# A two-block transformer kernel: memory tokens loaded in five parts between weights, zeros through TensorE first, modulation pieces moved between engines, constants in two loads

## The chip, the cores and the metric

The kernel runs on one core of a Trainium2 chip. The metric is the device time of one execution in microseconds. Three runs of the kernel before took 1735.03, 1736.86 and 1738.09 us; the median is 1736.86 us.

## What is computed

The reference is two transformer blocks over a sequence of 256 positions and 2048 features, in float32. The first block has adaptive modulation, then a wide projection, stick-breaking attention, retention, and an output projection. The second block has two layers that both attend to 256 memory tokens. What the change touches is this:

```
mod = silu(c) @ w_ada + b_ada              # c: (1, 2048), w_ada: (2048, 6144)
shift, scale, gate = split(mod, 3)
h = rms_norm(x, norm_gain) * (1 + scale) + shift
proj = h @ w_in
...
mem_n = rms_norm(mem, mem_norm_w)          # mem: (256, 2048)
k, v = mem_n @ w_mk, mem_n @ w_mv          # for both layers, width 512 each
```

The key and value products of the memory tokens depend on nothing else, so the kernel computes them first, while the modulation of the first block is being formed.

## The kernel before

Activations lie transposed: 16 tiles of 128 features by 256 positions. Every product is done in two parts of reduced float32: a matrix w is split into w_hi (ScalarE's copy, L429) and w_lo = w - w_hi (VectorE's subtraction, L433), and the activations likewise. Weights arrive in chunks of 512 KB, loaded by SyncE's queue (`load_weights`, L417) into a ring of 7 slots; a slot is loaded again when the chunk seven before it has been used. ScalarE and VectorE split a chunk three chunks ahead of TensorE (AHEAD = 3), and w_hi has 5 slots. `run_split` is the loop of ScalarE and VectorE over the chunks of a product, with a hook per chunk in which other work stands; `run_products` is TensorE's. When a block of a product ends, ScalarE copies its first half out of PSUM and VectorE adds the second (`take_product`, `add_product`); both wait there until TensorE has done the block's last chunk. Nothing is reordered: each engine executes its list as written, and semaphores tie the lists.

The first stage is G_MEM, four products of the memory tokens with 8 chunks each, so 32 chunks. The first and third have chunks of 2 tiles by 512 columns, and the weights are the moving side (L497 to L499, 12 matmuls of 512 columns a chunk); the second and fourth have chunks of 4 tiles by 256 columns, and the tokens are the moving side (L503 and L505). A unit u is the hook behind chunk u. On ScalarE and VectorE unit u comes after the split of chunk u + 3, on TensorE after the matmuls of chunk u.

Beside it run these:

- Memory tokens. SyncE loads them in four parts of four feature tiles (512 KB each), the first before weight 0, the others behind weights 0, 1 and 3; the constants (512.5 KB) come behind weight 4. ScalarE scales them by the gain (`mem_hi`, L808), VectorE makes the low parts (`mem_lo`, L1342). The first four tiles are made ahead of the first three splits, the others in units 0, 2 and 4. The root of the mean square is applied at the end, from sums: ScalarE squares four tiles at a time (`norm_square`, L712; units 0, 1, 3, 5), POOL sums three of the four groups (`add_squares`, L618 to L622), and TensorE sums over the partitions in unit 6 (`sum_squares`, L1998, L2002). The third and fourth squares wait for the POOL group two before them to be free.
- Modulation. For half 0, 32 pieces of w_ada (128 by 1024, 512 KB) are loaded by POOL's queue (L640) into a ring of 6 slots. A slot is loaded again once its piece has been used. VectorE multiplies a piece by its element of silu(c) and adds it to a sum (`ada_add`, L1332 for the first of each sum, L1335). Pieces 22, 23, 30 and 31 (DIRECT) go another way: TensorE multiplies them by a one-column operand in units 21, 22, 26 and 27 (`direct_columns`, L2022). VectorE adds one piece per unit from unit 3 to 27, and a second one in units 8, 13 and 18. In unit 28 TensorE turns the two sums into columns (`modulation_columns`, L2009).
- x. POOL loads x in four parts before pieces 10, 12, 14 and 16. ScalarE squares it in units 17, 19, 21 and 23; POOL sums before it issues pieces 22, 25 and 28; TensorE sums in unit 25; the inverse root is made in unit 26. In units 29, 30 and 31 ScalarE and VectorE make the first eight tiles of h (`half_norm`; on VectorE L1377 and L1378 for the modulation, L1226 for a tile's product, L1235 for its low part, on ScalarE L738 for the high part).

The next stage, 40 chunks, multiplies those eight tiles with w_in while the other half's 32 pieces come in. Its first two chunks need tiles 0 to 3.

## Time and profile before

| | |
|---|---|
| Median of three runs | 1736.86 us |
| The profiled execution | 1735.74 us |
| Its span | 1733.7 us |
| TensorE busy | 1694.3 us, 98% |
| VectorE busy | 1309.0 us, 76% |
| ScalarE busy | 905.9 us, 52% |
| GpSimd busy | 179.5 us, 10% |
| DMA | 357.00 MB, mean 206 GB/s |

Matmuls are pipelined, so a busy TensorE is not one at its peak: at half clock it is as busy as at full clock. The time of a matmul is the distance between the starts of two of them, not the duration in the row. In the timeline a row gives start, duration, engine, line, operation, output and inputs, shapes and count; the square brackets hold how long the engine was idle before it and which instruction or transfer ended that. Line numbers are those of the kernel before.

### The profile page before, as it was taken

Reading aid. Unit: us, or ns where it says so; the run is one execution under the profiler, and the core shown is the slowest. Engines: PE = TensorE matmul, PEld = TensorE weight load, DVE = VectorE, ACT = ScalarE, POOL = GpSimd, SP = SyncE. Lnnn points to the kernel's source line nnn. Section 1 sums busy time; section 2 is a strip of 40 time slices with the busy share of each in tenths; the row PEclk is TensorE's granted clock in tenths of the full one; section 3 lists DMA queues with packets and bytes.
Section 4 is the critical chain, followed back from the end, with each engine's and each line's share of the span. In section 5 each row is a group of like instructions: output and inputs, shape, how many; then the busy total and the mean of one; then the engine's idle time right before and its main releaser. Section 6 shows DMA issues by size and latency. Waiting matters only on the chain.

```text
span 1733.7 us, 24087 instructions
## 1 busy us (share of the span) xinstructions
PE 1694.3 (98%) x9511; PEld 1460.7 (84%) x9511; DVE 1309.0 (76%) x1633; ACT 905.9 (52%) x1178; POOL 179.5 (10%) x198
## 2 busy tenths in 40 slices
PE   7899999999999999999999999999999999999997
PEld 5788878888888888888888888888888888888886
DVE  6879999897798757887677779965566667778654
ACT  6344453445565446665445666744454455565543
POOL 4321101000110200111010010001111000000001
PEclk9999999999999999999999999999999999999999
DMA  9989979775555566667676556565666565444563
GB/s 354 384 301 342 349 239 325 257 259 152 159 166 182 185 192 185 192 183 220 175 226 195 160 168 172 185 192 186 190 190 183 170 197 144 135 140 127 171 193 110
DMA packets 312287, 357.00 MB, mean 206 GB/s; under 512 B 11632, under 2 KB 285168, under 8 KB 312176
## 3 DMA queue, kind: packets, MB, share of 16 engines
q1 hardware_dynamic: 295792, 296.24, 56.3%
q0 software_dynamic: 16384, 59.22, 9.9%
q8 instruction: 76, 1.25, 0.3%
q14 instruction: 35, 0.29, 0.1%
HBM read 353.29 MB, written 2.13 MB: 205 GB/s over the span
## 4 chain that ended last, share of the span: by engine, by line
PE 72%; DVE 15%; ACT 6%; issue 3%; DMA 2%; POOL 1%; SPq 0%; DVEq 0%; ACTq 0%
PE psG L503 40%; PE psG L505 20%; DVE w_lo L433 6%; ACT w_hi L429 3%; PE psG L497 2%; PE psG L499 2%; PE psG L498 2%; DMA raw<-in_mem_w 2%; DVE P L1282 1%; DVE P L1287 1%; PE psH L1992 1%; DVE W L1896 0%; PE psH L2022 0%; PE psH L2227 0%; DMA ada_ring<-in_w_ada 0%
## 5 line engine op out<-in xcount | busy, mean ns | idle before, releaser
L433 DVE TENSOR_TENSOR w_lo<-raw,w_hi 128x1024 fp32r<-128x1024 f32 (+1 forms) x560 | 691.5, 1247 | 203.9 <-ACT w_hi L429 202.2
L503 PE MATMUL psG<-xA,w_hi 128*128 128x512 f32 x2624 | 839.7, 401 | 3.2 <-ACT P L470 1.1
L429 ACT ACTIVATE w_hi<-raw 128x1024 fp32r<-128x1024 f32 (+1 forms) x560 | 569.1, 1041 | 215.4 <-PE psG L505 152.4
L505 PEld LDWEIGHTS psG<-xA,w_lo 128*128 128x128 f32 x2624 | 493.0, 188 | 114.8
L505 PE MATMUL psG<-xA,w_lo 128*128 128x256 f32 x2624 | 519.3, 278 | 0.0
L503 PEld LDWEIGHTS psG<-xA,w_hi 128*128 128x128 f32 x2624 | 404.0, 189 | 12.0 <-issue 6.5
L503 PE MATMUL psG<-yP,w_hi 128*128 128x512 f32 x960 | 302.2, 396 | 3.0 <-DVE P L1287 1.6
L505 PEld LDWEIGHTS psG<-yP,w_lo 128*128 128x128 f32 x960 | 180.4, 188 | 42.6
L505 PE MATMUL psG<-yP,w_lo 128*128 128x256 f32 x960 | 188.7, 278 | 0.0
L472 ACT ACTIVATE P<-psG 128x512 f32<-128x512 f32 (+2 forms) x103 | 60.8, 590 | 228.1 <-PE psG L505 228.1
L503 PEld LDWEIGHTS psG<-yP,w_hi 128*128 128x128 f32 x960 | 146.2, 189 | 3.7 <-DVE P L1287 1.8
L1282 DVE TENSOR_TENSOR P<-psG,P 128x512 f32<-128x512 f32 (+2 forms) x103 | 70.2, 682 | 101.9 <-ACT P L472 101.8
L618 POOL TENSOR_TENSOR W<-W 128x512 f32<-128x512 f32 x17 | 28.1, 1653 | 582.4 <-ACT W L712 582.3
L640 POOL DMA_DIRECT2D ada_ring<-in_w_ada x96 | 51.1, 533 | 295.2 <-DVE gate_sum L1335 115.6
L1335 DVE SCALAR_TENSOR_TENSOR ada_sum<-ada_ring,silc,ada_sum 128x1024 f32<-128x1024 f32 x56 | 75.3, 1348 | 0.0
L1307 DVE TENSOR_TENSOR xT<-psG,xT 128x512 f32<-128x512 f32 x30 | 20.7, 691 | 42.5 <-PE psG L505 42.0
L497 PE MATMUL psG<-w_hi,xA 128*128 128x512 f32 x128 | 51.4, 401 | 0.0
L499 PE MATMUL psG<-w_hi,xA 128*128 128x512 f32 x128 | 50.0, 390 | 0.0
L498 PE MATMUL psG<-w_lo,xA 128*128 128x512 f32 x128 | 49.9, 390 | 0.0
L503 PE MATMUL psG<-xQ,w_hi 128*128 128x512 f32 x144 | 45.3, 396 | 0.0
L497 PE MATMUL psG<-w_hi,xM 128*128 128x512 f32 x64 | 28.5, 445 | 14.2 <-DVE w_lo L433 11.7
L742 ACT ACTIVATE xA<-xT,vec 128x256 fp32r<-128x256 f32 x32 | 14.3, 501 | 51.6 <-DVE xT L1310 27.2
(352 smaller groups left out, 1752.2 us busy)
## 6 DMA issues: line engine op xcount, KB each, us to landing
raw<-in_w_in SPq DMA_DIRECT2D x360, 512.0 KB, 3.8
raw<-in_w_out SPq DMA_DIRECT2D x128, 512.0 KB, 3.5
ada_ring<-in_w_ada POOLq DMA_DIRECT2D x96, 512.0 KB, 6.4
raw<-in_mem_w SPq DMA_DIRECT2D x32, 512.0 KB, 10.6
raw<-in_w_uq SPq DMA_DIRECT2D x24, 384.0 KB, 3.4
raw<-in_w_ukv SPq DMA_DIRECT2D x32, 128.0 KB, 2.4
raw<-in_w_ukv SPq DMA_DIRECT2D x16, 256.0 KB, 3.3
P<-in_memT SPq DMA_DIRECT2D x4, 512.0 KB, 7.1
```

The costliest lines, as they stand in the source:

```text
L429: nc.scalar.activation(high(n), low(n, raw), ACT.Copy).then_inc(hi_ready, 1)
L433: nc.vector.tensor_tensor(low(n), low(n, raw), high(n), ALU.subtract).then_inc(lo_ready, 1)
L472: nc.scalar.activation(g.dst(b), product(g, b, 0), ACT.Copy).then_inc(copied, 1)
L497: nc.tensor.matmul(out, x_hi, hi[:, w], start=first, stop=False)
L498: nc.tensor.matmul(out, x_hi, lo[:, w], start=False, stop=False)
L499: last = nc.tensor.matmul(out, x_lo, hi[:, w], start=False, stop=end)
L503: nc.tensor.matmul(psG[:, bank + f, :], hi[:, w], x, start=first, stop=False)
L505: last = nc.tensor.matmul(psG[:, bank + f, S:2 * S], lo[:, w], x[:, 0:S], start=False, stop=end)
L618: pair(nc.gpsimd.tensor_tensor(a[:, 0:512], a[:, 0:512], a[:, 512:1024], ALU.add))
L640: pool.dma_start(ada_ring[slot][:, :], ada_rows(k, part, half)).then_inc(ada_loaded[slot], 16)
L1282: ins = v.tensor_tensor(out, product(g, b, 1), out, ALU.add)
L1335: v.scalar_tensor_tensor(out=out, in0=src, scalar=silc[:, k:k + 1], in1=out, op0=ALU.mult, op1=ALU.add).then_inc(ada_used, 1)
```

## The change

The memory tokens are loaded in five parts, of 2, 2, 4, 4 and 4 tiles; the first stands before weight 0 and one behind each of weights 0 to 3. ScalarE and VectorE make part 0, split chunk 0, make part 1, split chunk 1, make part 2, split chunk 2, make part 3; part 4 is made in unit 0. Only the first 256 of 1025 columns of the constants (ones and identity) are loaded behind weight 4; the others come behind con1, after the weights of G_SBQK. TensorE first runs 16 matmuls over a tile of zeros that VectorE sets. No piece goes directly through TensorE. ScalarE scales pieces 0 and 1 (the first of each sum) in unit 4; VectorE adds one piece per unit from unit 5 on and the last three behind the stage. ScalarE's squares of x stand in units 21, 23, 25 and 27, TensorE's sum in unit 30, the inverse root in unit 31. `modulation_columns` and the three steps of `half_norm` stand behind the stage. POOL's first issue waits for the load of tiles 8 to 11, as before, which is now the fourth part.

The diff, with a declaration of semaphore names left out:

```diff
@@ -72,6 +72,9 @@
...
 MEM_UNITS, EARLY_UNITS = 32, 40
+MEM_PIECES = (range(0, 2), range(2, 4), range(4, 8), range(8, 12), range(12, 16))
+SCALED_BY_ACT = 2
+WARM_UP = 16
 MEM_ROOT = 80
@@ -229,7 +232,7 @@
...
         loaded = {n: sem("loaded_" + n) for n in ("x", "vec", "con", "con1", "pos", "late")}
-        mem_loaded = [sem(f"mem_loaded{i}") for i in range(4)]
+        mem_loaded = [sem(f"mem_loaded{i}") for i in range(len(MEM_PIECES))]
         ada_loaded = [sem(f"ada_loaded{i}") for i in range(len(ADA_RING))]
@@ -237,7 +240,7 @@
...
             "rt_t0 rt_s rt_qk rt_D rt_z rt_at rt_o rt_os rt_vc rt_sq rt_var rt_ln rt_rs rt_y "
-            "f1_yz f1_y f1_hi f1_lo dt_step ada_direct ada_folded mem_col mem_k "
+            "f1_yz f1_y f1_hi f1_lo dt_step ada_folded mem_col mem_k "
             "cv_acc cv_tap cv_a cv_e cv_l cv_b cv_s cv_done xt xd_done "
@@ -368,16 +371,6 @@
...
         ADA_BEFORE = [max([i for i in range(m) if ADA_SLOT[i] == ADA_SLOT[m]], default=None) for m in range(3 * ADA_HALF)]
-        DIRECT = (22, 23, 30, 31)
-        ADA_ADDED = [m - sum(d < m for d in DIRECT) for m in range(3 * ADA_HALF + 1)]
-
-        def modulation_used(eng, m):
-
-            if m in DIRECT:
-                eng.wait_ge(q["ada_direct"], DIRECT.index(m) + 1)
-            else:
-                eng.wait_ge(ada_used, ADA_ADDED[m] + 1)
-
         ADA_COUNT = [ADA_SLOT[:m + 1].count(ADA_SLOT[m]) for m in range(3 * ADA_HALF)]
@@ -580,16 +573,20 @@
...
-            def load_memory(g):
-                sp.dma_start(mem_raw[:, 4 * g:4 * g + 4, :], io["memT"].rearrange("(t p) s -> p t s", p=NP)[:, 4 * g:4 * g + 4, :])\
-                  .then_inc(mem_loaded[g], 16)
+            early_con = slice(0, CON["rot64"])
+            late_con = slice(CON["rot64"], NCON)
+
+            def load_memory(i):
+                part = slice(MEM_PIECES[i][0], MEM_PIECES[i][-1] + 1)
+                sp.dma_start(mem_raw[:, part, :], io["memT"].rearrange("(t p) s -> p t s", p=NP)[:, part, :])\
+                  .then_inc(mem_loaded[i], 16)
...
-                if c in (0, 1, 3):
-                    load_memory((0, 1, 3).index(c) + 1)
+                if c < 4:
+                    load_memory(c + 1)
                 if c == 4:
-                    sp.dma_start(con[:, :], io["con"]).then_inc(loaded["con"], 16)
+                    sp.dma_start(con[:, early_con], io["con"][:, early_con]).then_inc(loaded["con"], 16)
@@ -597,6 +594,8 @@
...
                     sp.dma_start(con1[:, :], io["con1"]).then_inc(loaded["con1"], 16)
+                    sp.wait_ge(loaded["con"], 16)
+                    sp.dma_start(con[:, late_con], io["con"][:, late_con]).then_inc(loaded["con"], 16)
             out = io["out"].rearrange("(t p) s -> p t s", p=NP)
@@ -623,7 +622,7 @@
...
             X_QUARTERS = (10, 12, 14, 16)
-            pool.wait_ge(mem_loaded[2], 16)
+            pool.wait_ge(mem_loaded[3], 16)
             for m, (half, k, part) in enumerate(ADA_ORDER):
@@ -633,7 +632,7 @@
...
                 if ADA_BEFORE[m] is not None:
-                    modulation_used(pool, ADA_BEFORE[m])
+                    pool.wait_ge(ada_used, ADA_BEFORE[m] + 1)
                 if m in X_QUARTERS:
@@ -670,6 +669,7 @@
...
             landed(pool, G_CB)
+            pool.wait_ge(loaded["con"], 32)
             pool.dma_start(C("dup", S), io["con"][:, CON["dup"]:CON["dup"] + S]).then_inc(loaded["late"], 16)
@@ -784,10 +784,6 @@
...
-            def first():
-                for n in range(AHEAD):
-                    split_hi(act, n)
-
             def run(g, hook=no_hook, hook_first=True, before_taken=lambda: None):
@@ -801,10 +797,10 @@
...
-            def mem_hi(g):
-
-                act.wait_ge(mem_loaded[g], 16)
-                for t in range(4 * g, 4 * g + 4):
+            def mem_hi(i):
+
+                act.wait_ge(mem_loaded[i], 16)
+                for t in MEM_PIECES[i]:
                     f(xM[:, t, 0:S], mem_raw[:, t, :], ACT.Copy, scale=V("mem_norm", t)).then_inc(q["nm_hi"], 1)
@@ -814,23 +810,32 @@
...
-            mem_hi(0)
-            first()
+            for i in range(AHEAD):
+                mem_hi(i)
+                split_hi(act, i)
+            mem_hi(AHEAD)
+
+            def first_scaled(m):
+
+                act.wait_ge(ada_loaded[ADA_SLOT[m]], 16 * ADA_COUNT[m])
+                act.wait_ge(q["silc_step"], 2)
+                f(ada_sum[:, m, :], ada_ring[ADA_SLOT[m]][:, :], ACT.Copy, scale=silc[:, 0:1]).then_inc(ada_used, 1)
             def mem_hook_1(unit):
-                if unit in (0, 2, 4):
-                    mem_hi(unit // 2 + 1)
+                if unit == 0:
+                    mem_hi(AHEAD + 1)
                 if unit in (0, 1, 3, 5):
                     norm_square(0, (0, 1, 3, 5).index(unit), mem_raw)
+                if unit == 4:
+                    for m in range(SCALED_BY_ACT):
+                        first_scaled(m)
                 if unit == 7:
                     mem_root()
-                if unit in (17, 19, 21, 23):
+                if unit in (21, 23, 25, 27):
                     act.wait_ge(loaded["x"], 64)
-                    norm_square(1, (17, 19, 21, 23).index(unit), xT)
-                if unit == 26:
+                    norm_square(1, (21, 23, 25, 27).index(unit), xT)
+                if unit == 31:
                     norm_inverse_root(1)
-                if unit >= MEM_UNITS - 3:
-                    half_norm(0, unit - (MEM_UNITS - 3))
@@ -848,6 +853,8 @@
...
                 run(g, at_units(8 * i, mem_hook_1), hook_first=False)
+            for step in range(3):
+                half_norm(0, step)
             for i, g in enumerate((G_SBQK0, G_RTQK0, G_SBV0)):
@@ -877,7 +884,7 @@
...
             act.wait_ge(loaded["con1"], 16)
-            run(G_RTV, lambda b, p: sb_hook(2 + b, p), before_taken=lambda: act.wait_ge(ada_used, ADA_ADDED[3 * ADA_HALF]))
+            run(G_RTV, lambda b, p: sb_hook(2 + b, p), before_taken=lambda: act.wait_ge(ada_used, 3 * ADA_HALF))
@@ -1259,10 +1266,6 @@
...
                 return hook
-
-            def first():
-                for n in range(AHEAD):
-                    split_lo(dve, n)
@@ -1314,6 +1317,7 @@
...
+            link(v.memset(fold_to[:, :], 0.0))
             dve.wait_ge(q["silc_step"], 1)
@@ -1331,19 +1335,21 @@
...
                 else:
-                    dve.wait_ge(ada_used, ADA_ADDED[m] - (m < 2 * ADA_HALF))
+                    dve.wait_ge(ada_used, max(SCALED_BY_ACT, m - (m < 2 * ADA_HALF)))
                     v.scalar_tensor_tensor(out=out, in0=src, scalar=silc[:, k:k + 1], in1=out, op0=ALU.mult,
...
-            def mem_lo(g):
-
-                for t in range(4 * g, 4 * g + 4):
+            def mem_lo(i):
+
+                for t in MEM_PIECES[i]:
                     dve.wait_ge(q["nm_hi"], t + 1)
...
-            mem_lo(0)
-            first()
+            for i in range(AHEAD):
+                mem_lo(i)
+                split_lo(dve, i)
+            mem_lo(AHEAD)
@@ -1390,34 +1396,36 @@
...
                     if units == MEM_UNITS:
-                        done.append(done[-1] + (3 <= u < units - 4) + (u in (8, 13, 18)))
+                        done.append(done[-1] + (u >= 5))
                     else:
...
-            ADDED_0 = [m for m in range(ADA_HALF) if m not in DIRECT]
-
             def ada_hook(u0, units, half):
...
                         u = u0 + 8 * b + p // 2
-                        if units == MEM_UNITS and u in (0, 2, 4):
-                            mem_lo(u // 2 + 1)
+                        if units == MEM_UNITS and u == 0:
+                            mem_lo(AHEAD + 1)
                         for m in range(done[u], done[u + 1]):
-                            ada_add(ADA_HALF * half + m if half else ADDED_0[m])
+                            ada_add(ADA_HALF + m if half else SCALED_BY_ACT + m)
                         if half and u == 1:
...
                         if half and u == units - 5:
-                            dve.wait_ge(ada_used, ADA_ADDED[2 * ADA_HALF])
+                            dve.wait_ge(ada_used, 2 * ADA_HALF)
                             fold(ada_sum.rearrange("p c n -> p (c n)"), 2)
-                        if u >= units - 3:
+                        if half and u >= units - 3:
                             half_norm(half, u - (units - 3))
...
                 run(g, ada_hook(8 * i, MEM_UNITS, 0), hook_first=False)
+            for m in range(SCALED_BY_ACT + ada_units(MEM_UNITS)[-1], ADA_HALF):
+                ada_add(m)
+            for step in range(3):
+                half_norm(0, step)
             for i, g in enumerate((G_SBQK0, G_RTQK0, G_SBV0)):
@@ -1430,7 +1438,7 @@
...
             def gate_fold(half):
-                dve.wait_ge(ada_used, ADA_ADDED[2 * ADA_HALF + KT * (half + 1)])
+                dve.wait_ge(ada_used, 2 * ADA_HALF + KT * (half + 1))
                 fold(gate_sum[:, :], 1)
@@ -1669,6 +1677,7 @@
...
             run(G_SZ1, xdt_hook)
+            dve.wait_ge(loaded["con"], 32)
@@ -2011,29 +2020,21 @@
...
-            def direct_columns(i):
-
-                m = DIRECT[i]
-                half, k, part = ADA_ORDER[m]
-                pe.wait_ge(ada_loaded[ADA_SLOT[m]], 16 * ADA_COUNT[m])
-                pe.wait_ge(q["silc_step"], 2)
-                for t in range(8):
-                    c = KT * part + t
-                    ins = mm(psH[:, BD, c:c + 1], ada_ring[ADA_SLOT[m]][:, t * NP:t * NP + NP], silc[:, k:k + 1],
-                             start=i == 0 and t == 0, stop=False)
-                ins.then_inc(q["ada_direct"], 1)
+            def warm_up():
+
+                pe.wait_ge(dve_step, 1)
+                for _ in range(WARM_UP):
+                    mm(psH[:, BD, 0:NP], fold_to[:, :], fold_to[:, :], start=True, stop=True)
             def modulation_columns():
-                pe.wait_ge(ada_used, ADA_ADDED[ADA_HALF])
-                ada_columns(ada_sum[:, 0, :], 0, None, first=False)
+                pe.wait_ge(ada_used, ADA_HALF)
+                ada_columns(ada_sum[:, 0, :], 0, None)
                 ada_columns(ada_sum[:, 1, :], KT, "ada_cols", first=False)
...
                 mm(psH[:, BD, 0:32 * parts], fold_to[:, :], folded[:, 0:32 * parts], start=True, stop=True).then_inc(q[name], 1)
-
-            DIRECT_AT = (21, 22, 26, 27)
@@ -2048,15 +2049,13 @@
...
                     ins.then_inc(q["mem_col"], 1)
-                if u == 25:
+                if u == 30:
                     sum_squares(1)
-                if u in DIRECT_AT:
-                    direct_columns(DIRECT_AT.index(u))
-                if u == MEM_UNITS - 4:
-                    modulation_columns()
-
+
+            warm_up()
             for i, g in enumerate(G_MEM):
                 run_products(pe, g, lambda b, p: mem_tail_hook(i, p))
+            modulation_columns()
```

## Rows read from the trace of the kernel before

**Rows 1.** Busy time by stretch: stretch, length, engines with counts, PEclk, DMA share, GB/s.

```profile
9.43:25.81 16.38, 13.91 (x49) 10.89 (x49) 9.31 (x12) 11.48 (x17) 9.06 (x10) 0.99 1.06 385
...
40.93:127.72 86.79, 81.95 (x458) 70.47 (x459) 68.28 (x64) 36.37 (x45) 29.93 (x40) 0.98 0.97 350
127.72:239.35 111.63, 110.82 (x610) 95.46 (x609) 104.63 (x113) 51.34 (x63) 15.33 (x29) 1.00 0.95 323
```

**Rows 2.** Timeline of TensorE, first matmuls of chunks 8, 16, 24 and 32.

```profile
40.79 0.72 PE L503 MATMUL psG<-xM,w_hi 128*128 128x512 f32 x2
...
63.18 0.40 PE L497 MATMUL psG<-w_hi,xM 128*128 128x512 f32 x1
...
96.13 0.61 PE L503 MATMUL psG<-xM,w_hi 128*128 128x512 f32 x2
...
127.72 0.63 PE L503 MATMUL psG<-xA,w_hi 128*128 128x512 f32 x2
```

**Rows 3.** Timeline of TensorE, sums, waits and one-column passes.

```profile
35.54 0.59 PE L1998 MATMUL psH<-W,con 128*128 128x256 f32 x2
...
37.51 0.58 PE L497 MATMUL psG<-w_hi,xM 128*128 128x512 f32 x1
...
79.77 0.47 PE L497 MATMUL psG<-w_hi,xM 128*128 128x512 f32 x1 [0.90 <-DVE w_lo L433]
...
85.34 2.13 PE L2022 MATMUL psH<-silc,ada_ring 128*128 128x1 f32 x16 [2.58 <-DMA ada_ring<-in_w_ada]
...
91.56 1.84 PE L2022 MATMUL psH<-silc,ada_ring 128*128 128x1 f32 x16
...
115.79 3.63 PE L2009 MATMUL psH<-con,ada_sum 128*128 128x1 f32 x32
```

**Rows 4.** Timeline of TensorE, the first start and one restart.

```profile
9.43 0.76 PE L497 MATMUL psG<-w_hi,xM 128*128 128x512 f32 x1 [9.43 <-DVE w_lo L433]
...
15.42 0.40 PE L499 MATMUL psG<-w_hi,xM 128*128 128x512 f32 x1
...
25.81 0.80 PE L497 MATMUL psG<-w_hi,xM 128*128 128x512 f32 x1 [2.47 <-DVE xM L1342]
...
28.95 0.40 PE L498 MATMUL psG<-w_lo,xM 128*128 128x512 f32 x1
```

**Rows 5.** Timeline of ScalarE, splits of chunks 0, 5 and 19.

```profile
6.97 1.06 ACT L429 ACTIVATE w_hi<-raw 128x1024 fp32r<-128x1024 f32 x1 [0.17 <-DMA raw<-in_mem_w]
...
22.06 1.06 ACT L429 ACTIVATE w_hi<-raw 128x1024 fp32r<-128x1024 f32 x1 [2.38 <-DMA raw<-in_mem_w]
...
69.65 1.06 ACT L429 ACTIVATE w_hi<-raw 128x1024 fp32r<-128x1024 f32 x1 [2.24 <-DMA raw<-in_mem_w]
```

**Rows 6.** Timeline of all engines, squares of the memory tokens and their sums.

```profile
16.58 1.04 ACT L712 ACTIVATE W<-P 128x1024 f32<-128x1024 f32 x1
...
26.69 2.13 POOL L618 TENSOR_TENSOR W<-W 128x512 f32<-128x512 f32 x1 [0.58 <-ACT W L712]
...
30.05 1.61 POOL L622 TENSOR_TENSOR W<-W 128x256 f32<-128x256 f32 x1
...
31.69 1.06 ACT L712 ACTIVATE W<-P 128x1024 f32<-128x1024 f32 x1 [1.59 <-POOL W L622]
```

**Rows 7.** Timeline of VectorE and ScalarE, what the end is made of.

```profile
60.39 2.48 DVE L1335 SCALAR_TENSOR_TENSOR ada_sum<-ada_ring,silc,ada_sum 128x1024 f32<-128x1024 f32 x2
...
111.41 0.60 ACT L472 ACTIVATE memkv<-psG 128x512 f32<-128x512 f32 x1 [5.57 <-PE psG L505]
...
119.86 1.28 DVE L1226 SCALAR_TENSOR_TENSOR W<-xT,gs,W 128x256 f32<-128x256 f32 x3
```

**Rows 8.** Timeline of POOL and VectorE, one group of sums beside an add.

```profile
75.49 1.38 POOL L618 TENSOR_TENSOR W<-W 128x512 f32<-128x512 f32 x1 [1.51 <-ACT W L712]
75.64 2.31 DVE L1335 SCALAR_TENSOR_TENSOR ada_sum<-ada_ring,silc,ada_sum 128x1024 f32<-128x1024 f32 x1
...
78.49 0.57 POOL L640 DMA_DIRECT2D ada_ring<-in_w_ada x1
```

## The prediction

> **What bounds the kernel now.** I read the table of stretches first. From 127.72 us on TensorE is busy for 110.82 of 111.63 us, and the change hardly reaches that part: it moves later or earlier as a whole. Between 9.43 and 127.72 us, the memory products, TensorE has gaps while the 16 DMA engines are at a share of about 1.0 and move 385 GB/s in the first stretch [rows 1]. Then TensorE's timeline, to see where its time goes. The stage is 32 chunks of weights. I number them 0 to 31; chunk 8 starts at 40.79, chunk 16 at 63.18, chunk 24 at 96.13, and the stage ends at 127.72 us [rows 2]. A chunk without disturbance takes 22.39 / 8 = 2.80 us (chunks 8 to 15); a token-major one takes 12 matmuls of 0.228 us = 2.73 us.
>
> From 40.79 to 127.72 are 86.9 us for 24 chunks that need 8 x 2.80 + 8 x 2.73 + 8 x 2.80 = 66.6 us. The other 20.3 us are seen in the rows: four groups of one-column matmuls on modulation pieces (2.0 us, then 1.7 us each: 7.1), the 32 one-column passes that finish the sums (from 115.79, 3.63 in the row, 3.5 up to the next start), the sum of squares of x (2.0, as the one at 35.54 to 37.51), a wait of 2.7 us for a modulation piece before 85.34 with a slow restart behind it (1.6), and three short waits for weights, 0.6 to 0.9 us each (the last is shown), a little more in start-to-start time [rows 3]. Before 40.79: the first 13 matmuls run at 0.43 us against 0.23 us (512 columns at 1.2 and at 2.4 GHz, though the granted clock of the stretch reads 0.99; 2.7 us lost), a gap 22.95 to 25.81 (2.6 us), and 7 slow matmuls behind it (1.4 us) [rows 4].
>
> **The change part by part.**
>
> *Start.* The first load is 256 KB less, 0.7 us at 385 GB/s (512 KB: 1.36 us). Weight 0 was waited for until 6.97 us [rows 5], now about 6.3, and chunk 0 starts at 8.7 instead of 9.43. The sum of squares at 35.54, ten passes of 256 columns, takes 0.20 us a pass; so the 16 matmuls on zeros, two passes of 128 columns each, take 0.4 us apiece at the low clock and last some 6 us from about 1 us on. The low clock lasted 6.0 us after the first start (9.43 to 15.42, rows 4). I let the clock be high at 8.7, worth 2.7 us; at worst nothing is won. Chunks 1 to 6 then follow the landings: by pieces in SP's order, weight 5 is behind 10.25 pieces and 2 of POOL's instead of 11 and 2, so 21 instead of 22.06 us [rows 5]. With split (1.06) and subtraction (1.23) chunk 5 starts at 23.4, chunk 6 ends at 29.2 instead of 35.5 us.
>
> There TensorE must sum the squares of the memory tokens, and this is late next. The chain is ScalarE square, POOL sums, square, sums. POOL's third group began at 26.69, its last sum ended at 31.66, and the last square ran 31.69 to 32.75 [rows 6]. The first square waits in the new kernel for the load of tiles 12 to 15 and falls at 17.1 against 16.58 us; POOL's groups and the issues between them keep their order, so the third group again starts near 26.7. ScalarE's two scalings (2 x 1.04) stand between the third square and the fourth and fit into that POOL group. So the end of chunk 6 is followed by 2.5 us of idle to 31.7, then sums at the low clock (3.4 + 1.0 in place of 2.0 us), done 36.1; chunk 7 with a slow head: 3.1; the columns of the root 0.35: chunk 8 at 39.6, a gain of 1.2 us. The warm start's 2.7 us is spent in this wait. Bounds for the part: chain 1 us later and longer low clock, -0.5; chain done when TensorE arrives, +6.5 (chunk 8 at 34.3).
>
> *Middle.* The four pieces leave TensorE: 7.1 us, and the 2.7 + 1.6 us at 85 go with the wait for a piece. VectorE gets them less the two that ScalarE scales: 2 x 1.24 us, and adds one piece per chunk; split and add are 1.2 + 1.24 against 2.80 us. Are weights in time? By pieces: weight 19 was waited for until 69.65 [rows 5]. SP had queued 25 pieces to it, and POOL 4 of x and, by the code's slot rule (a slot is free when the piece six before it has been added; VectorE had added 15), some 19.7; 48.7 x 1.36 + 3.9 = 70.1. New: 24.25 + 4 + 17.7 = 45.95, so 66.4 + 2.3 for splitting = 68.7. TensorE gets to chunk 19 at 39.6 + 8 x 2.80 + 3 x 2.73 = 70.2. So the weights no longer hold it, with 1.5 us to spare, and the short waits go (2.6). From there a chunk asks for two pieces, 2.72 us. Chunk 31 ends at 39.6 + 66.6 + 2.0 (squares of x) = 108.2 us. Bound above: weights late by 2 us.
>
> *End.* Before, the final columns and the first part of x's normalization stood between chunks 28 and 31, and TensorE had three chunks to do. Now all of it stands behind chunk 31, bare. With T its end: ScalarE copies the last block (0.2 + 0.6), VectorE adds it (T + 1.5), then three pieces left over at 1.24 (60.39, two in 2.48) [rows 7]: T + 5.2. The columns at the low clock, 2.0/1.7 of 3.5 = 4.0: T + 9.2. VectorE's 0.4 for modulation, then three scalings in 1.28 and five more steps of 0.40 up to the low part of tile 3 [rows 7]: 4.5, T + 13.7. TensorE starts the next stage there, slow for half of its first 3 to 6 us, 1.4 to 2.8 lost (rows 4); I take 2.2. VectorE will be somewhat behind at T, since the pieces 22, 25 and 28 wait in POOL's queue behind x's squares, whose ScalarE units are 4 later: +0.7. Together 16.6 us against nothing.
>
> 108.2 + 16.6 = 124.8 against 127.72: 2.9 us gained.
>
> *Nothing for the rest.* The memset of zeros (under 0.3 us) is ahead of VectorE's wait for ScalarE. The constants in two loads take 0.75 of a piece from the beginning and put it, with SP's wait for the first load (long landed), behind con1's load, where 1.0 us of transfer meets weights that are up to seven chunks ahead: 0, at worst 1.0. POOL and VectorE wait for the second load several stages later; nothing stands behind those waits by then. POOL's first issue waits for the third long load, one piece later, 1.4 us; the squares come after it anyhow.
>
> *Clock.* The rows show full speed regained after 3.1 us in one place and 6.0 in another [rows 4]. The Trainium skill ("TensorE: Matmul & The Clock Gate", "What's actually happening") says that the point varies from run to run, one kernel having had 6, 11 or 14 slow matmuls. By its 6 to 14 a restart costs, as an estimate, 1.2 to 2.8 us at this kernel's 0.2 us each; with two new restarts the sum would be between 1 us better and 1 us worse. The two restarts in the rows have 7 and 13, and agree.
>
> **The rivals.** (a) *The squares are not late*, or the low clock is not entered in so short a wait. For: POOL's sums are shorter when VectorE is idle. Then weights bind: chunk 19 at 68.7, T = 106.7; 106.7 + 13.7 + 2.2 = 122.6, 5.1 us gained: 1731.8 for the measured median. (b) *VectorE is behind at the end: slower.* An add beside POOL's sums took 2.31 us for 1.24 (75.49 and 75.64) [rows 8]. POOL's second and third group for x, up to 5.0 us each (26.69 to 31.66, rows 6), come while VectorE has chunks 25 to 31 to do, after piece 22, which took from 78.49 to 85.3 to be there [rows 3, 8]. If each of six units costs 1.2 + 2.31 = 3.5 for 2.44, VectorE loses 6.4 us against a slack of about 1: 5.4 us later at T, and TensorE's start with it: 108.2 + 13.7 + 5.4 + 2.2 = 129.5, 1.8 us slower, 1738.7. It decides once the last of the three adds ends over 8.8 us after T (5.2 + 3.6). Against: POOL sums only half of that time. The Trainium skill ("GPSIMD Engine Reference", "Specifications") has VectorE instructions with two SBUF inputs contend with GpSimd, as these adds have; by it the case is real for all adds beside sums, and the trace agrees with 2.31 us. (c) *The change does not free TensorE*, since transfers hold it throughout: every piece still has to come, only 3 pieces fewer by chunk 19 (4 us). For: share 1.0 for 90 us. With weights 2 us late from there and the same end: 110.2 + 16.6 = 126.8, 0.9 us gained, 1736.0.
>
> **How the numbers follow.** The profiled execution took 1735.74 us, 2.0 around the span of 1733.7; the sum makes it 1732.8. The median of the three runs is 1.12 above it, 1736.86, so the forecast is 1734.0. Forecast 0.50, (a) 0.20, (b) 0.15, (c) 0.15. What can be told from no change is 0.2%, 3.5 us: faster needs 1733.4 or less. The forecast lies near that edge, and 0.4 of it falls beyond (0.20); (a) is beyond for nearly all of it (0.18), (c) hardly (0.02): faster 0.40. Slower than 1740.4 is (b) for half of it (0.08) and 0.02 of what I have not seen: 0.10. Same: 0.50. Own range of the forecast 1731.5 to 1737; with (a) and most of (b) 1728.5 to 1739.
>
> **What would show it.** Chunk 0 near 8.7 us at 0.23 us a matmul; a gap of TensorE after 29 us until POOL's and ScalarE's squares at 31.7, with slow matmuls behind; chunk 8 near 39.6; no wait for a weight over 0.5 us from there to chunk 31, end near 108; then about 14 us with nothing but 4 us of one-column passes, and the next stage at 122.6 with slow first matmuls; from there all rows as before, 3 us earlier. Wrong would be: chunk 8 before 36 (a), VectorE's last add later than 116 (b), waits for weights in chunks 16 to 25 (c), or a changed length from the next stage to the end.

## The result, and the profile after

The changed kernel takes 1741.01 us (median of 14 runs) against 1736.94 us for the kernel before (14 runs on the same chip): a ratio of 1.0022, interval 1.0014 to 1.0029. It is 4.1 us, 0.2%, slower; the forecast was 1734.0 us, 2.9 us faster. In a second set of runs, of the unchanged files, it was 1741.83 against 1737.38 us, 1.0027 (1.0017 to 1.0036). One execution of the changed kernel had a granted clock of 0.65 from end to end and took 2398.96 us; it is left out, and the profile shown here is of an execution in the second set.

Its page, the span and the busy times:

```profile
span 1738.9 us, 24035 instructions
...
PE 1697.5 (98%) x9479; PEld 1463.2 (84%) x9479; DVE 1311.2 (75%) x1636; ACT 908.2 (52%) x1180; POOL 179.8 (10%) x198
```

The span is 5.2 us longer than the 1733.7 us of before. The table of stretches of the changed kernel, columns as in [rows 1]: the first loads, the last eight chunks of the memory products, the end of that stage, and the stage behind it.

```profile
9.43:30.00 20.57, 20.43 (x84) 16.75 (x84) 14.82 (x21) 15.88 (x24) 11.66 (x12) 0.92 1.07 378
84.00:108.00 24.00, 22.88 (x126) 19.56 (x125) 24.00 (x18) 13.41 (x16) 16.52 (x17) 1.00 1.07 375
108.00:130.00 22.00, 10.16 (x49) 9.58 (x48) 14.85 (x23) 4.33 (x10) 3.17 (x6) 0.66 0.65 238
130.00:240.00 110.00, 109.18 (x590) 94.02 (x589) 100.53 (x105) 48.28 (x58) 15.33 (x29) 0.97 0.92 316
```

The reader sees three things. From 84 to 108 us VectorE has no idle time at all (24.00 of 24). From 108 to 130 us TensorE is busy for 10.16 of 22 us, at a granted clock of 0.66; before, it was busy from 108 us to the end of the stage, 127.72, at full clock. From 136 us on hardly anything differs: span less start of the next stage is 1733.7 - 127.72 = 1606.0 us before and 1738.9 - 129.52 = 1609.4 us after, and 2.8 of the 3.4 us more lie in the first 6 us of it: the matmuls that take from 129.52 to 135.60 in the rows below took 3.3 us before. So nearly the whole question lies ahead of 136 us. TensorE's timeline of the changed kernel, the rows that answer to [rows 2 to 4]:

```profile
1.05 6.11 PE L2027 MATMUL psH<-fold_to 128*128 128x128 f32 x32 [1.05 <-DVE fold_to L1320]
9.57 0.76 PE L490 MATMUL psG<-w_hi,xM 128*128 128x512 f32 x1 [2.41 <-DVE w_lo L426]
...
12.69 0.40 PE L491 MATMUL psG<-w_lo,xM 128*128 128x512 f32 x1
...
31.90 0.67 PE L2007 MATMUL psH<-W,con 128*128 128x256 f32 x2 [1.54 <-POOL W L621]
32.90 3.56 PE L2011 MATMUL psH<-W,con 128*128 128x256 f32 x8 [0.33 <-ACT W L712]
...
39.51 0.72 PE L496 MATMUL psG<-xM,w_hi 128*128 128x512 f32 x2
...
61.90 0.40 PE L490 MATMUL psG<-w_hi,xM 128*128 128x512 f32 x1
...
84.22 0.62 PE L496 MATMUL psG<-xM,w_hi 128*128 128x512 f32 x2
...
90.33 0.70 PE L496 MATMUL psG<-xM,w_hi 128*128 128x512 f32 x2 [0.38 <-DVE w_lo L426]
...
110.30 0.40 PE L498 MATMUL psG<-xM,w_lo 128*128 128x256 f32 x2
117.94 6.99 PE L2018 MATMUL psH<-con,ada_sum 128*128 128x1 f32 x32 [7.24 <-DVE ada_sum L1339]
129.52 1.19 PE L496 MATMUL psG<-xA,w_hi 128*128 128x512 f32 x2 [4.60 <-issue]
...
134.77 0.99 PE L496 MATMUL psG<-xA,w_hi 128*128 128x512 f32 x2
135.60 0.40 PE L498 MATMUL psG<-xA,w_lo 128*128 128x256 f32 x2
```

Chunk 8 starts at 39.51, chunk 16 at 61.90, chunk 24 at 84.22 us: TensorE is then 11.9 us ahead of before (96.13, [rows 2]). Chunk 31 ends at 110.70 us (110.30 + 0.40), 17.0 us ahead of the 127.72 of before, since the columns and two of the one-column pieces no longer stand in front of its end. From there TensorE does nothing but 32 one-column passes until 129.52 us, and the first matmuls of the next stage, up to 135.60, run at half speed. The 17.0 us and 4.6 more are given back behind chunk 31: 18.8 us up to the next stage and 2.8 us at its slow head.

VectorE's timeline of the changed kernel behind chunk 31, and one pair of rows from the stretch ahead of it:

```profile
87.23 1.87 POOL L617 TENSOR_TENSOR W<-W 128x512 f32<-128x512 f32 x1
87.87 2.32 DVE L426 TENSOR_TENSOR w_lo<-raw,w_hi 128x1024 fp32r<-128x1024 f32 x1
...
112.42 1.27 DVE L1339 SCALAR_TENSOR_TENSOR ada_sum<-ada_ring,silc,ada_sum 128x1024 f32<-128x1024 f32 x1
113.62 0.68 DVE L1285 TENSOR_TENSOR memkv<-psG,memkv 128x512 f32<-128x512 f32 x1
114.22 3.66 DVE L1339 SCALAR_TENSOR_TENSOR ada_sum<-ada_ring,silc,ada_sum 128x1024 f32<-128x1024 f32 x3
124.96 0.17 DVE L1383 TENSOR_TENSOR mod<-psH,vec 128x16 f32<-128x16 f32 x1 [7.08 <-PE psH L2018]
...
125.37 1.28 DVE L1233 SCALAR_TENSOR_TENSOR W<-xT,gs,W 128x256 f32<-128x256 f32 x3
```

VectorE has three instructions to finish when TensorE ends (the add that began at 110.09, the subtraction behind it and the add at 112.42), so the block's add, which waits for TensorE alone, starts only at 113.62. Then the three pieces left over, then it waits 7.08 us for the columns.

### The profile page after: what moved, and what is told of

It reads as the page before. It is cut to its first block, busy times and chain, and to the rows that moved or that the text cites. A ratio compares the mean times of both kernels' runs of the same rounds, so it can differ in the third digit from the quotient of the medians.

```text
span 2397.0 us, 24035 instructions
## 1 busy us (share of the span) xinstructions
PE 2373.3 (99%) x9479; PEld 1801.4 (75%) x9479; DVE 1314.5 (55%) x1636; ACT 911.9 (38%) x1180; POOL 165.8 (7%) x198
## 4 chain that ended last, share of the span: by engine, by line
PE 99%; DVE 0%; issue 0%; DMA 0%; ACT 0%; SPq 0%; DVEq 0%
PE psG L496 54%; PE psG L498 27%; PE psG L491 3%; PE psG L490 3%; PE psG L492 3%; PE psH L2001 1%; PE psH L2192 0%; PE psH L2213 0%; PE psH L2294 0%; PE psH L2226 0%; PE psH L2293 0%; PE psH L2305 0%; PE psH L2095 0%; PE psH L2018 0%; PE psH L2194 0%
## 5 line engine op out<-in xcount | busy, mean ns | idle before, releaser
L496 PE MATMUL psG<-xA,w_hi 128*128 128x512 f32 x2624 | 1114.1, 514 | 5.4 <-issue 4.6
L498 PEld LDWEIGHTS psG<-xA,w_lo 128*128 128x128 f32 x2624 | 543.6, 207 | 282.6 <-issue 54.2
L498 PE MATMUL psG<-xA,w_lo 128*128 128x256 f32 x2624 | 670.5, 344 | 0.0
L496 PEld LDWEIGHTS psG<-xA,w_hi 128*128 128x128 f32 x2624 | 513.6, 221 | 24.7 <-issue 14.9
L496 PE MATMUL psG<-yP,w_hi 128*128 128x512 f32 x960 | 399.8, 507 | 0.0
L498 PEld LDWEIGHTS psG<-yP,w_lo 128*128 128x128 f32 x960 | 198.9, 207 | 104.1 <-issue 19.2
L498 PE MATMUL psG<-yP,w_lo 128*128 128x256 f32 x960 | 244.1, 344 | 0.0
L496 PEld LDWEIGHTS psG<-yP,w_hi 128*128 128x128 f32 x960 | 187.2, 221 | 0.2
L490 PE MATMUL psG<-w_hi,xA 128*128 128x512 f32 x128 | 66.4, 518 | 0.0
L492 PE MATMUL psG<-w_hi,xA 128*128 128x512 f32 x128 | 65.0, 508 | 0.0
L496 PE MATMUL psG<-xM,w_hi 128*128 128x512 f32 x128 | 53.6, 509 | 0.0
```

The costliest lines, as they stand in the source:

```text
L490: nc.tensor.matmul(out, x_hi, hi[:, w], start=first, stop=False)
L492: last = nc.tensor.matmul(out, x_lo, hi[:, w], start=False, stop=end)
L496: nc.tensor.matmul(psG[:, bank + f, :], hi[:, w], x, start=first, stop=False)
L498: last = nc.tensor.matmul(psG[:, bank + f, S:2 * S], lo[:, w], x[:, 0:S], start=False, stop=end)
```

## The experiments

All runs are of one core and in rounds against the kernel before, whose median was 1736.9 to 1737.4 us in each set. In short, with the start of the next stage (the first matmul on xA) and whether that is at full speed. The last two columns are of one profiled execution each, which was up to 2.8 us faster (e6) and up to 1.5 us slower (e10) than the median, so differences of 1 to 2 us between two rows of them show little by themselves:

| kernel | median us | ratio to before (interval) | next stage at | its speed |
|---|---|---|---|---|
| before | 1736.94 | 1 | 127.72 | full |
| e1: the changed kernel | 1741.83 | 1.0027 (1.0017 to 1.0036) | 129.52 | half |
| e2: before, bare end | 1742.67 | 1.0031 (1.0020 to 1.0042) | 130.79 | half |
| e3: changed, no zeros | 1740.83 | 1.0019 (1.0009 to 1.0028) | 130.83 | half |
| e4: before, new loads | 1737.63 | 1.0002 (0.9992 to 1.0011) | 127.92 | full |
| e5: changed, zeros at the end | 1737.85 | 1.0005 (0.9997 to 1.0014) | 126.56 | full |
| e6: changed, end inside | 1733.43 | 0.9979 (0.9970 to 0.9989) | 121.93 | full |
| e7: changed, no pieces left over | 1738.84 | 1.0008 (0.9999 to 1.0017) | 126.35 | half |
| e8: changed, squares of x early | 1741.81 | 1.0029 (1.0017 to 1.0040) | 131.13 | half |
| e9: e7 with zeros | 1735.72 | 0.9991 (0.9983 to 1.0000) | 127.29 | full |
| e10: e6, second adds later | 1735.22 | 0.9989 (0.9980 to 0.9998) | 128.03 | full |
| e11: before, no one-column pieces | 1732.60 | 0.9973 (0.9962 to 0.9984) | 123.15 | full |
| e12: e11, ScalarE scales two | 1735.08 | 0.9989 (0.9978 to 1.0001) | 125.15 | full |

Span less start of the next stage is 1606.0 to 1607.7 us for all that start it at full speed, and up to 3.7 us more for the others.

**e1: the changed kernel again.**

> The changed kernel as it is, for its profile. Theory A (the bare end is dearer than predicted): chunk 31 of the memory products ends near 108 us, but the next stage starts at 126 to 130 us, behind a gap of 18 us or more; everything before is as forecast. Theory B (the gain before the end is missing): chunk 31 ends at 112 us or later, the gap is 14 to 16 us. Theory C (a later stage pays): the next stage starts at 122 to 124 us as forecast, and the loss of 4 us stands behind it, in the 40 chunks with the other half's pieces or where the rest of the constants is loaded.

Measured: 1741.83 us; its rows are those above. The loss is repeated. It is theory A, with some of B: the gap behind chunk 31 is 18.8 us and the next stage starts at 129.52 us, and chunk 31 is 2.5 us late. Theory C fell.

**e2: the kernel before with the bare end alone.**

```diff
-                if unit >= MEM_UNITS - 3:
-                    half_norm(0, unit - (MEM_UNITS - 3))
...
                 run(g, at_units(8 * i, mem_hook_1), hook_first=False)
+            for step in range(3):
+                half_norm(0, step)
...
-                if u == MEM_UNITS - 4:
-                    modulation_columns()
...
                 run_products(pe, g, lambda b, p: mem_tail_hook(i, p))
+            modulation_columns()
```

> The kernel before, with only the columns of the modulation and the first eight tiles of h moved behind the memory products. Theory A: slower by 10 us or more (nothing earlier is gained, the end is bare: columns 0.5 us dearer, 4.5 us of VectorE's first tiles, 2 to 3 us of low clock, wait for the last block's copy and add 1.5 us), some 9 to 12 us. Theory C: the same 9 to 12 us. If the end is cheaper than I think, under 6 us.

Measured: 5.3 us more than before, 1.0031 (1.0020 to 1.0042) of it. That is not the 9 to 12 us expected, but its last case, an end cheaper than thought, under 6 us. It has TensorE's timeline

```profile
122.56 3.63 PE L2011 MATMUL psH<-con,ada_sum 128*128 128x1 f32 x32
130.79 1.19 PE L503 MATMUL psG<-xA,w_hi 128*128 128x512 f32 x2 [4.60 <-issue]
```

Here the pieces are all added when TensorE arrives, so the columns follow at once and at full speed (3.63 us). Still 4.60 us of idle follow, VectorE's and ScalarE's first tiles, and then a start at half speed. So a bare end without late adds and without slow columns costs 5.3 us here: more than the whole forecast gain.

**e3: the changed kernel without the 16 matmuls on zeros.**

```diff
-            warm_up()
             for i, g in enumerate(G_MEM):
```

> The changed kernel without the 16 matmuls on zeros. By the prediction the warm start is spent in the wait for the squares of the memory tokens, so nothing changes: within 1 us of the changed kernel. The rival, that the start is worth its 2.7 us, has it 2.5 to 3 us slower than the changed kernel.

Measured: 1740.83 us, 1.0 us less than with the zeros, and the intervals overlap: the zeros bring nothing. TensorE's timeline:

```profile
8.56 0.77 PE L490 MATMUL psG<-w_hi,xM 128*128 128x512 f32 x1 [8.56 <-DVE w_lo L426]
...
31.63 0.67 PE L2007 MATMUL psH<-W,con 128*128 128x256 f32 x2 [0.96 <-POOL W L621]
32.63 1.99 PE L2011 MATMUL psH<-W,con 128*128 128x256 f32 x8 [0.33 <-ACT W L712]
...
37.55 0.72 PE L496 MATMUL psG<-xM,w_hi 128*128 128x512 f32 x2
```

The sum waits for POOL at 31.63 us as it did at 31.90 with the zeros. The next eight passes took 1.99 us, not 3.56, and chunk 8 starts 2.0 us earlier than in e1. That can't be put down to the missing zeros. The kernels e5 to e10 below have the zeros and the same code as e1 up to chunk 8. In e7, e9 and e10 the eight passes took 1.99 us as well, behind 1.84, 1.53 and 1.48 us of idle, and chunk 8 started at 37.62, 38.05 and 38.52 us. In e5, e6 and e8 they took 3.12, 3.68 and 3.65 us, behind 1.49, 1.88 and 1.51 us, and chunk 8 started at 39.10, 39.81 and 40.32 us. Which clock follows a wait of this length changes from one execution to the next. In e3 the 2.0 us are gone again by the end of the stage (next stage at 130.83 us): TensorE waits 3.9 us for VectorE's low parts between 40 us and the end, against 1.1 in e1. What the runs show is that the sum waits for POOL with the zeros and without them, so a warm start has nothing to gain up to there.

**e4: the kernel before with the new loads alone** (five parts between the weights, constants in two loads; the fifth part shares the semaphore of con1).

```diff
+MEM_PIECES = (range(0, 2), range(2, 4), range(4, 8), range(8, 12), range(12, 16))
...
-                if c in (0, 1, 3):
-                    load_memory((0, 1, 3).index(c) + 1)
+                if c < 4:
+                    load_memory(c + 1)
...
-            mem_hi(0)
-            first()
+            for i in range(AHEAD):
+                mem_hi(i)
+                split_hi(act, i)
+            mem_hi(AHEAD)
```

> The kernel before, with only the five loads of memory tokens, their order on ScalarE and VectorE, and the constants in two loads; one load's semaphore is shared with a later one. By the prediction the squares come at the same time and the sum waits for them, so the gain is 0 to 1.5 us. Rival: the transfers saved (0.75 of a piece, 1 us) and the earlier start carry through to 4 us, since weights bind in chunks 16 to 22. Rival on the other side: the late constants cost 1 us where con1 is loaded.

Measured: 1.0002 (0.9992 to 1.0011). The new order of loads is worth nothing by itself, and costs nothing.

**e5: the changed kernel with zeros around the columns.** 30 zero matmuls ahead of the columns and 18 behind them; nothing is on TensorE's list there but the wait. VectorE overwrites the tile of zeros one unit later than in e1, since it is needed longer.

```diff
+            zeros(30, BD)
             modulation_columns()
+            zeros(18, BA)
```

> The changed kernel with 30 more matmuls on zeros between chunk 31 and the modulation columns and 18 between the columns and the next stage (and the tile of zeros overwritten one unit later). Theory A, the low clock at the bare end costs some 6.5 us (columns 7.0 instead of 3.5 us, first chunks of the next stage 3.1 us lost): columns in 3.5 us, next stage at full speed, 5 to 6.5 us faster than the changed kernel, about 1735.5. Rival, the waits themselves are the loss and the clock only a symptom of the trace: within 1 us of the changed kernel. Second rival, zeros do not raise the clock or are dropped in the wait of 4.6 us: 3.5 us at most.

Measured: 1737.85 us, 4.0 us less than e1, with the same work late on the same engines. TensorE's timeline:

```profile
109.93 6.86 PE L2031 MATMUL psH<-fold_to 128*128 128x128 f32 x60
117.32 3.73 PE L2018 MATMUL psH<-con,ada_sum 128*128 128x1 f32 x32 [0.53 <-DVE ada_sum L1339]
120.91 5.89 PE L2031 MATMUL psH<-fold_to 128*128 128x128 f32 x36
126.56 0.70 PE L496 MATMUL psG<-xA,w_hi 128*128 128x512 f32 x2
```

The columns take 3.73 us instead of 6.99, and the first matmuls of the next stage run at full speed. So 3.3 us in the columns and about 3 us at the head of the stage were the low clock alone; against that sum of 6.3 us the medians show 4.0. About 1.0 of the difference is that the last zeros are still running when the first tile is ready (120.91 + 4.60 = 125.5 us), for these 36 passes took 0.16 us each, partly at the low clock; the rest is not accounted for. The expectation, 5 to 6.5 us, was missed by 1 us.

**e6: the changed kernel with its end inside the stage again**: squares, root, columns and first tiles in the units of before, and seven second adds so that no piece is left over.

```diff
-                        done.append(done[-1] + (u >= 5))
+                        done.append(done[-1] + (5 <= u < 28) + (u in (8, 11, 14, 17, 20, 23, 26)))
...
-                        if half and u >= units - 3:
+                        if u >= units - 3:
                             half_norm(half, u - (units - 3))
...
+                if u == MEM_UNITS - 4:
+                    modulation_columns()
```

> The changed kernel with its end put back as it was before: squares of x in units 17 to 23, sum in 25, root in 26, columns in 28, the eight tiles in units 29 to 31; VectorE adds two pieces in seven units so that all are added by unit 27. Theory A, the move of the end behind the stage is the loss: the next stage starts at 116 to 120 us, 8 to 11 us faster than the kernel before, about 1727. Rival, VectorE (pieces it did not have before, beside POOL's sums) or the transfers can't deliver 32 pieces by then: the stage ends at 124 us or later, 1733 or more.

Measured: 1733.43 us, 8.4 us less than e1 and 0.9979 (0.9970 to 0.9989) of before: the loss becomes a gain. TensorE's timeline:

```profile
108.31 3.90 PE L2016 MATMUL psH<-con,ada_sum 128*128 128x1 f32 x32 [0.61 <-DVE ada_sum L1339]
...
121.93 0.63 PE L496 MATMUL psG<-xA,w_hi 128*128 128x512 f32 x2
```

All that the changed kernel lost was in where its end stands and in the pace of adds that goes with it; this run does not tell these two apart. The expectation, next stage at 116 to 120 us and 1727 us, was too good: in this trace TensorE waits 4.8 us for low parts on the way, and runs at the low clock for 3.4 us twice, once of it right behind the columns (from 112.08 us).

**e7: the changed kernel with no pieces left over**, the end still bare.

```diff
-                        done.append(done[-1] + (u >= 5))
+                        done.append(done[-1] + (5 <= u < 32) + (u in (13, 17, 21)))
```

> The changed kernel with the three leftover pieces added as second ones in units 13, 17 and 21, so that none stands behind the stage. If the leftover adds are on the path, 3.7 us less between chunk 31 and the columns, and 3 to 4 us faster than the changed kernel, about 1737.5. Rival, VectorE is behind anyhow from chunk 24 on and what it does not do at the end it does before: under 1 us.

Measured: 1738.84 us, 3.0 us less than e1, as expected if the adds were on the path; but the rows show another cause. TensorE's and VectorE's timelines:

```profile
114.89 0.40 PE L498 MATMUL psG<-xM,w_lo 128*128 128x256 f32 x2
117.43 4.32 PE L2018 MATMUL psH<-con,ada_sum 128*128 128x1 f32 x32 [2.15 <-DVE ada_sum L1339]
126.35 1.19 PE L496 MATMUL psG<-xA,w_hi 128*128 128x512 f32 x2 [4.60 <-issue]
```

```profile
116.10 1.27 DVE L1339 SCALAR_TENSOR_TENSOR ada_sum<-ada_ring,silc,ada_sum 128x1024 f32<-128x1024 f32 x1
117.30 0.68 DVE L1285 TENSOR_TENSOR memkv<-psG,memkv 128x512 f32<-128x512 f32 x1
```

The columns start at 117.43 us, hardly earlier than in e1 (117.94): chunk 31 now ends at 115.29 instead of 110.70, with 6.8 us of waits for VectorE's low parts against 1.1, since VectorE has three adds more to do before it. The adds are only moved; VectorE ends them at the same time. What is gained is the clock: TensorE idles 2.15 us ahead of the columns, not 7.24, and they take 4.32 us, not 6.99.

The same trace has the warm start that e1 lacked, and a sum of squares at full speed behind a longer wait than e1's 1.54 us:

```profile
8.58 0.47 PE L490 MATMUL psG<-w_hi,xM 128*128 128x512 f32 x1 [2.13 <-DVE w_lo L426]
8.88 0.40 PE L491 MATMUL psG<-w_lo,xM 128*128 128x512 f32 x1
...
31.69 0.67 PE L2007 MATMUL psH<-W,con 128*128 128x256 f32 x2 [1.84 <-POOL W L621]
32.69 1.99 PE L2011 MATMUL psH<-W,con 128*128 128x256 f32 x8 [0.33 <-ACT W L712]
```

**e8: the changed kernel with the squares of x in the units of before** and POOL's sums two or three pieces earlier. Of the edit, POOL's part:

```diff
-                if m in (22, 25, 28):
-                    add_squares(1, [(22, 25, 28).index(m)])
+                if m in (20, 22, 25):
+                    add_squares(1, [(20, 22, 25).index(m)])
```

> The changed kernel with x's squares in units 17 to 23 (POOL's sums before pieces 20, 22 and 25, TensorE's sum in unit 25, root in 26), nothing else. If POOL's sums beside VectorE's work in chunks 24 to 31 are what makes chunk 31 end at 110.5 instead of 108.2 and VectorE 3 us late behind it: chunk 31 ends at 108 to 109, the columns start 2 to 4 us earlier, total 2 to 4 us less. Rival, they slow VectorE the same wherever they stand: under 1 us.

Measured: 1741.81 us, as e1; chunk 31 ended at 112.61 us and the columns started at 119.55, both later than in e1. POOL's sums now ran from 72.29 to 92.64 us instead of 82.22 to 100.30, still beside splits and adds. So it is not their place beside the last adds that makes the end late; how much they cost VectorE over the whole stage isn't tested.

**e9: e7 with zeros**, 8 matmuls ahead of the columns and 14 behind, and the tile of zeros overwritten one unit later, as in e5.

```diff
+            zeros(8, BD)
             modulation_columns()
+            zeros(14, BA)
```

> The changed kernel with both: no pieces left over (second adds in units 13, 17, 21) and zeros in the waits of the end (8 matmuls before the columns, 14 behind them). If the bare end is leftover adds + low clock + VectorE's first tiles, the two add up: next stage starts near 125.5 us at full speed, 6 to 7 us faster than the changed kernel and 2 to 3 us faster than the kernel before, about 1734.5. If they overlap (the clock is low only because of the adds): no better than the better of the two, 1738.

Measured: 1735.72 us, 3.1 us less than e7 and 6.1 less than e1: the two effects add up roughly (3.0 and 4.0 alone). The next stage starts at full speed at 127.29 us. The columns took 5.06 us here, so part of them ran at the low clock, though TensorE had idled for only 0.37 us ahead of them, behind 16 passes over zeros; that isn't explained.

**e10: e6 with the second adds later**, in units 15, 17, 19, 21, 23, 25 and 26 (the edit against e6).

```diff
-                        done.append(done[-1] + (5 <= u < 28) + (u in (8, 11, 14, 17, 20, 23, 26)))
+                        done.append(done[-1] + (5 <= u < 28) + (u in (15, 17, 19, 21, 23, 25, 26)))
```

> The kernel with the end inside the stage, with the second pieces per unit later: units 15, 17, 19, 21, 23, 25 and 26 instead of 8 to 26 in steps of three. If transfers bind in chunks 16 to 24 (ScalarE waits 19.7 us for weights there), asking for pieces later frees them for weights: chunks 16 to 19 come earlier, but the columns must not be later than 108.3: 1 to 2 us faster. Rival, VectorE binds at the end and the pieces come too late: columns at 110 or later, 1 to 3 us slower.

Measured: 1735.22 us, 0.9989 (0.9980 to 0.9998) of before: 1.8 us slower than e6, with intervals that overlap. The first expectation was missed and the rival came true, in its place and its size: the columns came at 111.18 us. Waits and timeline of TensorE:

```profile
PE psG L490 <- DVE w_lo L426: 5.1, 6, 1.6
PE psH L2016 <- DVE ada_sum L1339: 3.7, 1, 3.7
```

```profile
111.18 6.64 PE L2016 MATMUL psH<-con,ada_sum 128*128 128x1 f32 x32 [3.68 <-DVE ada_sum L1339]
```

VectorE's work is bunched ahead of the columns, TensorE waits for it, and the 3.68 us of idle bring the low clock: 6.64 us for the passes.

**e11: the kernel before, the four one-column pieces given to VectorE**, and nothing else.

```diff
-        DIRECT = (22, 23, 30, 31)
+        DIRECT = ()
...
-                        done.append(done[-1] + (3 <= u < units - 4) + (u in (8, 13, 18)))
+                        done.append(done[-1] + (3 <= u < units - 4) + (u in (8, 10, 13, 15, 18, 20, 23)))
...
-                ada_columns(ada_sum[:, 0, :], 0, None, first=False)
+                ada_columns(ada_sum[:, 0, :], 0, None)
...
-            DIRECT_AT = (21, 22, 26, 27)
+            DIRECT_AT = ()
```

> The kernel before with only the four one-column pieces moved from TensorE to VectorE (second adds in units 8, 10, 13, 15, 18, 20 and 23), the end where it was. If this is the one part that pays: 7.1 us of TensorE less, of which the transfers and VectorE leave some 4: the same as the kernel with the end inside, about 1733.4, since the start was worth nothing. Rival, the start pays once TensorE is less loaded: 1 us or less faster than before here.

Measured: 1732.60 us, 0.9973 (0.9962 to 0.9984) of before. It has the lowest time of all, and beats both kernels: by 4.8 us the one before, by 9.2 us the changed one of e1. Its timeline and waits of TensorE:

```profile
109.65 3.63 PE L2009 MATMUL psH<-con,ada_sum 128*128 128x1 f32 x32
113.14 1.05 PE L503 MATMUL psG<-xM,w_hi 128*128 128x512 f32 x2
...
123.15 0.63 PE L503 MATMUL psG<-xA,w_hi 128*128 128x512 f32 x2
```

```profile
PE psG L497 <- DVE w_lo L433: 3.8, 4, 1.6
PE psG L503 <- DVE w_lo L433: 2.1, 1, 2.1
```

The columns start 6.1 us earlier than in [rows 3] and run at full speed. Of the 7.1 + 4.3 us that left TensorE, 4.6 are seen at 123.15 us. Of the other 6.8 us, 3.6 are in waits for VectorE's low parts from 40 us on, 5.9 us now for 2.3 before. Nearly all of the rest is the low clock. TensorE had it from 92.68 to 96.32 us, behind the wait of 2.1 us, and from 113.14 to 116.87 us, right behind the columns and with no idle time ahead of it; each stretch cost about 1.7 us. Before, the matmuls behind the same columns (119.28 us) ran at full speed.

**e12: e11, and ScalarE scales pieces 0 and 1** as in the change; six second adds (the edit against e11).

```diff
+                if unit == 4:
+                    for m in range(SCALED_BY_ACT):
+                        first_scaled(m)
...
-                        done.append(done[-1] + (3 <= u < units - 4) + (u in (8, 10, 13, 15, 18, 20, 23)))
+                        done.append(done[-1] + (4 <= u < units - 4) + (u in (8, 11, 14, 17, 20, 23)))
```

> The kernel before without the one-column pieces, and ScalarE scaling pieces 0 and 1 in unit 4 (VectorE adds from unit 4 to 27, second pieces in units 8, 11, 14, 17, 20 and 23). If VectorE is what holds the stage, its 1.5 us less make it 0.5 to 1.5 us faster than the kernel without this part, about 1731.5. If transfers hold it, the same, 1732.6, within 0.5 us.

Measured: 1735.08 us, 0.9989 (0.9978 to 1.0001). Two instructions less on VectorE are no gain here; against e11 it is 2.5 us more, with intervals that overlap, and neither case of the expectation. In the traces the next stage starts 2.0 us later: TensorE had the low clock for 10.2 us between 40 us and there, against 6.8 in e11, which is 1.7 us of loss, and waited 6.3 us against 5.9. Whether the changed order of the second adds brings this on, or chance does, is open.

## Why the prediction was wrong, step by step

**Start: right in its sum, in part by luck.** Chunk 0 started at 9.57, not 8.7, for weight 0 was there at 7.11 us, not 6.3 (6.10 in e3, 6.12 in e7). Its first seven matmuls ran at half speed: the zeros ended at 7.16 us and TensorE then idled for 2.41 us, so the warm start, put at 2.7 us, was not there; in e7 it was. The prediction had that gain spent in the wait for the squares, and so it was: the sums at 31.90 (forecast 31.7), chunk 8 at 39.51 (forecast 39.6). That the wait swallows the start is shown by e3 (no zeros, no loss) and by e7, e9 and e10; e4 shows that the loads alone do nothing. That the sums ran at the low clock behind the wait, as forecast, was luck: they did in e1, e5, e6 and e8 and did not in e3, e7, e9 and e10, where chunk 8 came 1 to 2 us sooner. Rival (a) fell as to the squares; its other half, no low clock behind so short a wait, came true in four of the eight.

**Middle: right to chunk 24, then short.** Chunk 16 at 61.90 as forecast, chunk 24 at 84.22 for 83.8, and no wait for a weight: rival (c) fell. Then chunk 31 ended at 110.70 instead of 108.2 us, 2.5 late. I had VectorE's load per chunk at 1.2 + 1.24 = 2.44 us and saw the 0.36 left of 2.80 as room; VectorE was busy for 24.00 of 24 us, single instructions of 1.2 us took 2.3 beside POOL's sums, and TensorE waited for a low part three times (0.38 us at 90.33, and two like it, 1.1 us together). Of the remaining 1.4 us, 0.4 were there at chunk 24; the rest isn't traced. The sum that T rests on had a gap of its own: the named parts of its 20.3 us come to 19.5, and it lets all 20.3 go except the squares and the columns. The wait for low parts is the mechanism of rival (b), in the place given, at under half of its price of 5.4 us: the last leftover add ended 7.2 us after chunk 31 (114.22 + 3.66), short of the 8.8 from which it was to decide. The Trainium skill ("GPSIMD Engine Reference", "Specifications") names this contention for VectorE's instructions with two SBUF inputs; the 2.32 us of the subtraction at 87.87, beside POOL's sum at 87.23, agree.

**End: the step that failed.** The mechanism was right (a bare end of columns, tiles and a slow start), its size was not. By its terms, forecast against the profile of e1:

| term | forecast us | measured us | off |
|---|---|---|---|
| chunk 31 ends (T) | 108.2 | 110.7 | +2.5 |
| T to the columns | 5.2 + 0.7 | 7.2 | +1.3 |
| columns | 4.0 | 7.0 | +3.0 |
| VectorE's first tiles | 4.5 | 4.6 | +0.1 |
| lost at the slow head | 2.2 | 2.8 (129.52 to 135.60, less the 3.3 us of before) | +0.6 |
| sum | 124.8 | 132.3 | +7.5 |

132.3 against 127.72 is 4.6 us slower in the trace; the medians have 4.1 to 4.4. The largest single error is the columns: 4.0 us forecast, 7.0 measured. I took their slowdown from one row in which one-column passes had followed 2.58 us of idle, 2.0 us for 1.7 [rows 3]. The runs give the same 32 passes after different idle times:

| idle of TensorE ahead of them | 32 one-column passes | from |
|---|---|---|
| 0 | 3.63 to 3.73 us | before, e2, e4, e11, e12 |
| 0.37 | 5.06 | e9, behind zeros |
| 0.53 and 0.61 | 3.73 and 3.90 | e5 (behind zeros), e6 |
| 2.15 | 4.32 | e7 |
| 3.68 | 6.64 | e10 |
| 6.95 to 7.25 | 6.99 | e1, e3, e8 |

After a wait as long as this one the whole group was slow in all three traces, 0.218 us a pass for 0.11, and not only its beginning. Behind shorter waits the time doesn't follow the idle time alone (e9), as it didn't at the sums. My row was one of the case in between. I had written that the start of the next stage would be slow and did not carry the same thought to the columns ahead of it. e5 takes away the low clock and gets 4.0 us back: that part of the loss is shown. e6 moves the end inside, with the adds that belong to it, and gains 8.4, the whole of it.

**What the parts are worth**, from the runs: the four one-column pieces off TensorE, -4.8 us (e11 against before); the bare end, +5.3 (e2 against before) and 8.4 on the changed kernel, where the late adds and the low clock in the columns come with it (e1 against e6); loads 0 (e4); zeros first 0, or 1.0 worse (e3); ScalarE's two scalings no gain (e12). So I found the gain and where it would be given back, and came out 7 us too low. About half of that is two sizes in the end, columns and slow head, drawn from rows with a shorter wait than the one that I had just worked out myself (+3.6); the other half is a later chunk 31 and later columns behind it (+3.8), of which the 1.1 us of waits for low parts and the 1.3 us behind chunk 31 are VectorE's. The range, up to 1739.0, was closed too early above: its upper end is rival (b) at 1738.7 with columns of 4.0 us, and with 7.0 it would have been 1741.7. That e7 starts its columns no earlier than e1 shows a second thing: the three leftover adds, 3.7 us on my path, were not a cost of where they stood, since VectorE was busy throughout from chunk 24 on. The parts don't add up by themselves: -4.8 and +5.3 make 0.5, and the change measured +4.1. In e1's trace the other 3.6 us are where the parts meet: VectorE, with the pieces that left TensorE and no second adds, ends late, so TensorE idles 7.24 us ahead of its columns and runs them at the low clock. No run tests that remainder alone. Not settled either is why e12 is not faster than e11.
